# A two-block transformer kernel: the two norms around the first residual summed in four partition blocks, the first attention head's start reordered, and one buffer fill spread over two heads

## The reference, cut to what matters

```python
x = x + _rms_norm(mix, norm_post_mix[i])      # y = mix * rsqrt(mean(mix^2) + eps) * g
h = _rms_norm(x, norm_pre_ffn[i])
hid = h @ ffn_up                               # 1024 -> 2 * 2816
```

```python
q = (rms_norm(q_lat, g_qa) @ w_qb)             # per head 64 plain + 32 rotary columns
kv = (rms_norm(kv_lat, g_kva) @ w_kvb)         # per head 64 key + 64 value columns
q = concat([q_nope, rope(q_pe)]); k = concat([k_nope, broadcast(rope(k_pe))])
p = softmax(q @ k^T * scale); o = p @ v
```

## Time and profile before

| | us |
|---|---|
| median of 3 runs | 1794.77 |
| lowest and highest | 1790.65 to 1795.23 |
| the profiled execution | 1791.69 |
| its span, first to last instruction | 1789.8 |
| PE busy | 1745.0 (97%) |
| POOL, DVE, ACT busy | 954.3, 1026.1, 763.2 |
| mean granted clock of TensorE | 0.993 of full speed |

### The profile page before, as it was taken

How to read it: one execution, slowest core, us unless ns; L and a number is a source line. 1 busy time by engine, 2 the same in 40 slices (tenths; PEclk the granted TensorE clock), 3 DMA queues, 4 the chain that set the end, 5 groups by cost and what they waited for, 6 DMA issues and landing times.

```text
span 1789.8 us, 24548 instructions
## 1 busy us (share of the span) xinstructions
PE 1745.0 (97%) x9450; PEld 1401.5 (78%) x9450; DVE 1026.1 (57%) x1312; ACT 763.2 (43%) x1261; POOL 954.3 (53%) x758
## 2 busy tenths in 40 slices
PE   8999999999899999999998999999999999999997
PEld 7677999877488888887787777776867888888776
DVE  4697544576755555201455666667485666666575
ACT  4553766423333333101433565567124444444562
POOL 3443777757088999999356022224544444444062
PEclk9999999999999999999999999999999999999998
DMA  5121000224112222424111000001231111111221
GB/s 190 71 94 48 2 1 2 96 104 170 56 70 97 101 105 95 165 105 166 48 48 71 24 24 1 24 0 60 106 153 48 42 48 47 49 47 48 77 71 47
DMA packets 18861, 126.24 MB, mean 71 GB/s; under 512 B 2096, under 2 KB 2352, under 8 KB 4304
## 3 DMA queue, kind: packets, MB, share of 16 engines
q1 hardware_dynamic: 18624, 124.41, 18.8%
q10 hardware_dynamic: 144, 0.52, 0.1%
HBM read 122.83 MB, written 2.10 MB: 70 GB/s over the span
## 4 chain that ended last, share of the span: by engine, by line
PE 64%; issue 15%; POOL 11%; DVE 7%; ACT 2%; DMA 0%; POOLq 0%; ACTq 0%; SPq 0%; DVEq 0%
POOL w_hi L648 8%; PE banks L903 6%; PE banks L1231 5%; PE banks L1210 4%; PE banks L1382 4%; PE banks L1385 4%; PE banks L1383 4%; POOL w_lo L639 3%; PE banks L769 3%; PE banks L1093 3%; PE banks L1098 3%; PE banks L1094 3%; PE banks L1437 2%; PE banks L751 2%; PE banks L752 2%
## 5 line engine op out<-in xcount | busy, mean ns | idle before, releaser
L648 POOL TENSOR_TENSOR w_hi<-raw,der 128x512 fp32r<-128x512 f32 x296 | 342.6, 1168 | 462.1 <-PE banks L1385 187.3
L639 POOL TENSOR_TENSOR w_lo<-raw,w_hi 128x512 fp32r<-128x512 f32 x336 | 467.0, 1402 | 67.2 <-ACT w_hi L1528 67.2
L751 PE MATMUL banks<-h_hi,w_hi 128*128 128x512 f32 x496 | 197.5, 398 | 2.4 <-DVE h_lo L2363 2.2
L752 PE MATMUL banks<-h_lo,w_hi 128*128 128x512 f32 x496 | 193.2, 389 | 0.0
L753 PE MATMUL banks<-h_hi,w_lo 128*128 128x512 f32 x496 | 193.1, 389 | 0.0
L1382 PE MATMUL banks<-h_hi,w_hi 128*128 128x512 f32 (+1 forms) x384 | 145.5, 379 | 0.0
L1383 PE MATMUL banks<-h_lo,w_hi 128*128 128x512 f32 (+1 forms) x384 | 130.6, 355 | 0.0
L2011 ACT ACTIVATE dP<-banks,der 128x768 f32<-128x768 f32 x64 | 57.7, 902 | 160.8 <-DVE der L2767 160.8
L751 PEld LDWEIGHTS banks<-h_hi,w_hi 128*128 128x128 f32 x496 | 93.1, 188 | 31.9 <-issue 8.8
L1385 PE MATMUL banks<-h_hi,w_lo 128*128 128x512 f32 (+1 forms) x384 | 116.0, 356 | 0.0
L698 POOL TENSOR_TENSOR Of<-Of,Ls 128x768 f32<-128x768 f32 x8 | 14.6, 1831 | 186.9 <-DVE Ls L2569 186.9
(11 more groups left out here) (491 smaller groups left out, 4229.3 us busy)
## 6 DMA issues: line engine op xcount, KB each, us to landing
raw<-in_stream SPq DMA_DIRECT2D x84, 1024.0 KB, 4.8
ada_raw<-in_ada_w SPq DMA_DIRECT2D x18, 1024.0 KB, 6.9
raw<-in_ada_w SPq DMA_DIRECT2D x4, 1024.0 KB, 4.8
xT<-in_x_t SPq DMA_DIRECT2D x2, 1024.0 KB, 6.5
xT<-in_x_t SPq DMA_DIRECT2D x1, 2048.0 KB, 7.6
ada_end<-in_ada_w SPq DMA_DIRECT2D x2, 1024.0 KB, 5.8
out_t<-z SPq DMA_DIRECT2D x8, 256.0 KB, 2.1
ctxT<-in_ctx_t SPq DMA_DIRECT2D x1, 1024.0 KB, 7.1
```

What stands on the lines that cost most here:

```text
L639: return pool.tensor_tensor(lo[:, h, part(i), :], raw_tiles(half)[:, part(i), :], hi[:, h, part(i), :], ALU.subtract)
L648: pool.tensor_tensor(hi[:, h, part(i), :], raw_tiles(half)[:, part(i), :], one, ALU.mult).then_inc(hi_done, 1)
L751: pe.matmul(banks[b][:, :], hi, tile(rhs_hi, k), start=(at_k == 0), stop=False)
L752: pe.matmul(banks[b][:, :], hi, tile(rhs_lo, k), start=False, stop=False)
```

## The change

Norms: the squares of 7 tiles are added in `nacc`; the sum over partitions is made in four blocks of 128 tokens, each on 32 partitions (`block_sums`: four matmuls with 32 columns of ones), first of `nacc`, then of the eighth square directly from `nt`, whose tile ACT now squares before it copies it. Root and reciprocal are then taken of 128x128 numbers (`brs`), and `spread_blocks` brings them back to 512 columns in bank 5 with four matmuls, from where DVE reads them. The second norm is made likewise. Ada blocks 6 and 7 follow the first spread, block 8 stands between the fourth and the fifth square, and block 9 is cut in two halves around the second spread. The first block of the feed-forward projection is written out ahead of the loop: for each k the three matmuls of tile 0 and of tile 1. The four mask columns that the spread uses get columns of their own (`MASK`).

Attention: `tops(0, t)` stand behind k = 0 to 4 of `mla_in(11)` and `row(0)` behind k = 6. ACT's `row_copy(0)` comes before the last gate and `query_hi(1)`; its two `KHI[1]` copies move behind `weigh_keys(0, 2)`, and the two `KLO[1]` copies, formerly on DVE, behind `weigh_keys(0, 3)`. DVE takes all five reductions of head 0 before `rope_query(1)`; the fill of the second pair is cut into `fill_zeros` and `fill_ones`, for buffer 0 in head 0 and buffer 1 in head 1, and `query_lo(1)` moves behind `top(1, 0)`. PE's `query(2, 0)` moves ahead of `tops(1, 0)`.

```diff
@@ ada_blocks, PE
-        def ada_blocks(blocks):
+        def ada_blocks(blocks, parts=range(KT)):
...
-                for k in range(KT):
+                for k in parts:
...
@@ PE, the norms and the first feed-forward block
-        pe.wait_ge(out_summed, KT)
-        pe.matmul(banks[4][:, :], ones, nacc[:, :], start=True, stop=True).then_inc(post_sum, 1)
+        def block_sums(at, squares, first, last):
+            for j in range(4):
+                mm = pe.matmul(banks[4][32 * j:32 * j + 32, at:at + P], ones[:, 0:32], squares[:, P * j:P * j + P], start=first, stop=last)
+            return mm
+        def spread_blocks(root):
+            for j in range(4):
+                mm = pe.matmul(banks[5][:, P * j:P * j + P], der[:, MASK + j:MASK + j + 1].broadcast_to([P, P]), root, start=True, stop=True)
+            return mm
+        pe.wait_ge(out_summed, KT - 1)
+        block_sums(0, nacc, True, False)
+        pe.wait_ge(out_sq, KT)
+        block_sums(0, nt[:, 1, :], False, True).then_inc(post_sum, 1)
+        pe.wait_ge(post_root, 2)
+        spread_blocks(brs[:, 0, :]).then_inc(post_sum, 1)
         ada_blocks((6, 7))
         for k in range(KT):
+            if k == CT:
+                ada_blocks([8])
             pe.wait_ge(pre_sq, k + 1)
-            pe.matmul(banks[5][:, :], ones, nt[:, k % 2, :], start=(k == 0), stop=(k == KT - 1)).then_inc(pre_sq_read, 1)
-        ada_blocks((8, 9))
+            block_sums(P, nt[:, k % 2, :], k == 0, k == KT - 1).then_inc(pre_sq_read, 1)
+        ada_blocks([9], range(CT))
+        pe.wait_ge(pre_root, 2)
+        spread_blocks(brs[:, 1, :]).then_inc(pre_sq_read, 1)
+        ada_blocks([9], range(CT, KT))
+        n = STREAM["up"]
+        s = half_of(n)
+        pe.wait_ge(split_full, n + 1)
...
+        for k in range(KT):
+            pe.wait_ge(nh_ready, k + 1)
+            for j in range(2):
...
+                pe.matmul(b[:, :], hi, h1_hi[:, k, :], start=(k == 0), stop=False)
+                pe.matmul(b[:, :], hi, h1_lo[:, k, :], start=False, stop=False)
+                mm = pe.matmul(b[:, :], lo, h1_hi[:, k, :], start=False, stop=(k == KT - 1))
...
@@ PE, attention
-            if k in (0, 2, 3, 5, 6):
-                tops(0, (0, 2, 3, 5, 6).index(k))
-        row(0)
+            if k < 5:
+                tops(0, k)
+            if k == 6:
+                row(0)
...
+                if h == 0 and j == 0:
+                    query(after, 0)
@@ ACT, norms
-            if m < 2 * KT - 1:
+            if m % KT < KT - 1:
                 act.activation(out, banks[bank][:, :], ACT.Copy).then_inc(out_copied, 1)
...
-        act.activation(nr[:, :], banks[4][:, :], ACT.Sqrt, scale=1.0 / D, bias=der[:, 127:128]).then_inc(post_root, 1)
+        act.activation(brs[:, 0, :], banks[4][:, 0:P], ACT.Sqrt, scale=1.0 / D, bias=der[:, 127:128]).then_inc(post_root, 1)
...
@@ DVE, norms
-            chain.link(dve.reciprocal(nr[:, :], nr[:, :]))
+            dve.reciprocal(brs[:, 0, :], brs[:, 0, :]).then_inc(post_root, 1)
+            dve.wait_ge(post_sum, 2)
...
@@ DVE, attention
         for h in range(A_HEADS):
             nxt, after = h + 1, h + 2
             if nxt < A_HEADS:
                 top(nxt, 0)
+            if h == 0:
+                query_lo(1)
...
             if nxt < A_HEADS:
                 top(nxt, 1)
+            if h < 2:
+                fill_zeros(1, h)
...
             if nxt < A_HEADS:
                 top(nxt, 3)
+            if h < 2:
+                fill_ones(1, h)
```

More of the change, by code:

```diff
@@ L1044, in _ @@
+        n = STREAM["up"] + 1
+        project([2 * half_of(n), 2 * half_of(n) + 1], half_of(n), n, n // 2 + 1, h1_hi, h1_lo)
+        with pe.Fori(0, N_UP // 2 - 1) as i:
             for u in range(2):
                 s = half_of(STREAM["up"] + u)
-                n = 2 * i + (STREAM["up"] + u)
-                project([2 * s, 2 * s + 1], s, n, i + (STREAM["up"] + u) // 2 + 1, h1_hi, h1_lo, ready=None if u else nh_ready)
+                n = 2 * i + (STREAM["up"] + 2 + u)
+                project([2 * s, 2 * s + 1], s, n, i + (STREAM["up"] + 2 + u) // 2 + 1, h1_hi, h1_lo)
@@ L1275, in _ @@
                 if after < A_HEADS:
-                    if j in (0, 2):
+                    if j in (0, 2) and h + j:
                         query(after, j // 2)
@@ L1726, in _ @@
         act.wait_ge(pre_sq_read, KT)
-        act.activation(nr[:, :], banks[5][:, :], ACT.Sqrt, scale=1.0 / D, bias=der[:, 127:128]).then_inc(pre_root, 1)
+        act.activation(brs[:, 1, :], banks[4][:, P:2 * P], ACT.Sqrt, scale=1.0 / D, bias=der[:, 127:128]).then_inc(pre_root, 1)
         for k in range(KT):
@@ L1892, in _ @@
         query_copy(1)
+        row_copy(0)
         mla_gate(11)
         query_hi(1)
-        for e in range(2):
-            ins = act.activation(KHI[1][e][rope_rows(e), :], KHI[0][e][rope_rows(e), :], ACT.Copy)
-        ins.then_inc(kpe_high.sem, 1)
-        row_copy(0)
         weigh_keys(0, 0)
@@ L1910, in _ @@
             weigh_keys(h, 2)
+            if h == 0:
+                for e in range(2):
+                    ins = act.activation(KHI[1][e][rope_rows(e), :], KHI[0][e][rope_rows(e), :], ACT.Copy)
+                ins.then_inc(kpe_high.sem, 1)
             if h == A_HEADS - 1:
@@ L1913, in _ @@
             weigh_keys(h, 3)
+            if h == 0:
+                act.wait_ge(*kpe_low.at(1))
+                for e in range(2):
+                    ins = act.activation(KLO[1][e][rope_rows(e), :], KLO[0][e][rope_rows(e), :], ACT.Copy)
+                ins.then_inc(kpe_low.sem, 1)
             if h == A_HEADS - 1:
@@ L2418, in _ @@
         dve.wait_ge(pre_root, 1)
-        chain.link(dve.reciprocal(nr[:, :], nr[:, :]))
+        dve.reciprocal(brs[:, 1, :], brs[:, 1, :]).then_inc(pre_root, 1)
+        dve.wait_ge(pre_sq_read, KT + 1)
         for k in range(KT):
@@ L2504, in _, with fill_zeros, fill_ones @@
                                  op0=ALU.mult, op1=ALU.mult).then_inc(lat_normed, 1)
-        def fill(i):
-            for e in range(2):
-                c = slice(96, 128) if e == 0 else slice(0, 32)
-                dve.memset(KHI[i][e][c, :].bitcast(F32), 0.0)
-                dve.memset(KLO[i][e][c, :].bitcast(F32), 0.0)
-                ins = dve.memset(VV[i][e][:, :, 64 - 64 * e:128 - 64 * e], 1.0)
-            chain.link(ins)
-            for e in range(2):
-                ins = dve.memset(KHI[i][e][top_at(e):top_at(e) + 1, :].bitcast(F32), 1.0)
-            ins.then_inc(mla_filled.sem, 1)
+        def fill_zeros(i, e):
+            c = slice(96, 128) if e == 0 else slice(0, 32)
+            dve.memset(KHI[i][e][c, :].bitcast(F32), 0.0)
+            dve.memset(KLO[i][e][c, :].bitcast(F32), 0.0)
+            chain.mark(dve.memset(VV[i][e][:, :, 64 - 64 * e:128 - 64 * e], 1.0))
+        def fill_ones(i, e):
+            chain.wait()
+            dve.memset(KHI[i][e][top_at(e):top_at(e) + 1, :].bitcast(F32), 1.0).then_inc(mla_filled.sem, 1)
         dve.wait_ge(*kpe_high.at(1))
@@ L2528, in _ @@
             dve.memset(qf[e][swap_rows(e), :], 0.0)
-        fill(0)
+        fill_zeros(0, 0)
+        fill_zeros(0, 1)
+        fill_ones(0, 0)
+        fill_ones(0, 1)
         def rope_query(h):
@@ L2574, in _ @@
         query_lo(0)
+        for t in range(5):
+            top(0, t)
         rope_query(1)
         rope_query_sum(1)
-        for t in range(5):
-            top(0, t)
         dve.wait_ge(block_done, BLK_LAST + 1)
-        fill(1)
-        query_lo(1)
-        for e in range(2):
-            r = rope_rows(e)
-            ins = dve.tensor_copy(KLO[1][e][r, :], KLO[0][e][r, :])
-        ins.then_inc(kpe_low.sem, 1)
         for h in range(A_HEADS):
```

51 lines of the change are left out of this document (29 added, 22 removed).

## The result

The changed kernel takes 1781.70 us in the median of five runs (1781.49 to 1783.92), the kernel before 1794.77 (1790.63 to 1795.23) beside it. The ratio is 0.9937, with a 95% interval from 0.9924 to 0.9950: faster by 0.6%, and inside the range, 0.7 us above its lower end. A later repeat gave 1783.6 (ratio 0.9942, 0.9927 to 0.9957). The profiled execution took 1783.92 us, its span 1781.8 against 1789.8.

The account below looks back on a forecast made before the run. PE's queue was taken to bound the kernel; norms 5.1 us (6.8 less 1.7 for the clock) plus attention 3.9 (5.6 less 1.7) gave 9.0, 1782.7 us, plus 3.1 for the median: 1785.8, range 1781 to 1790.5.

Parts of the forecast that it names:

- What bounds the kernel: Whole kernel: PE, busy 97% of the span, sets the end, so gains on its queue at either place reach the end.
- Short form of the norms: Norms to first feed-forward block: DVE's products start 3.3 us earlier, `nh` 2.2, block ends 487.4 not 494.2; 6.8 us gained.
- The clock at the first norm: First norm, ada blocks 6 and 7: one fall to half speed for 3.4 us costs 1.7, leaving the norms 5.1 us.
- rival 1: First norm: the clock does not fall, so the gain is 10.7 us, 1784.1; chance 0.25.
- Head 0: Start of attention's heads: scores start 3.6 us earlier, full clock kept, `tops(1, 1)` at 982.5 instead of 988.05; 5.6 us gained.
- What is given back: Heads 0 and 1: DVE's memsets and rotary steps delay reductions by 0.8 us a head, 1.7 with row-copy delay; attention 3.9.
- Rival 3: Heads 0 and 1: DVE's fills cost 2.3 us per head, not 0.8; attention 0.9, together 6.0, 1788.8; chance 0.10.
- The sum: Whole kernel: norms 5.1 plus attention 3.9 gives 9.0 us; 1782.7 from the profiled execution, 1785.8 as median; chance 0.42.
- Rival 4: Norms: head start lost on PE's queue, `nh` at 475.0, block ends no earlier than 490.5; 5.0 us in all, 1789.8; chance 0.10.
- rival 5: First norm: the clock falls and ada products don't restore it; `nh` near 488.7, 5.1 us slower or up to 1800.5; chance 0.05.

Follow-up runs that it names:

- gap_filled: Changed kernel with the first four of ada block 8's eight matmuls moved ahead of PE's wait for the first spread; median 1783.3 us, ratio 0.9941.
- longer_idle: Changed kernel with a second 128x128 reciprocal on DVE ahead of the first norm's own, lengthening PE's gap; median 1784.65 us, ratio 0.9948.
- not_interleaved: Changed kernel with the first feed-forward block back in the loop, all of tile 0 before tile 1; median 1787.2 us, ratio 0.9966.
- row_copy_late: Changed kernel with ACT's row_copy(0) again behind the last gate and query_hi(1), key copies left as changed; median 1788.2 us, ratio 0.9966.
- fills_on_gpsimd: Changed kernel with the second pair's fills taken from DVE and put on POOL behind its split; median 1779.6 us, ratio 0.9922.
- before_again: The kernel before, unedited, run once more for a second trace; norms' interval 42.47 us instead of 41.54, heads' interval 52.28.
- again: The changed kernel, unedited, run once more as the reference; 1783.6 us, ratio 0.9942.

## Why the prediction was right, step by step

**What bounds the kernel.** Right. PE's queue is the late one at the norms: a gap filled in it came out whole in the interval (`gap_filled`), a gap widened in it as well (`longer_idle`). That the gains reach the end is borne out by the corrected spans, to some 1 us.

**Short form of the norms.** Right to 0.3 us at these steps, when the trace's start is shifted by the 0.9 us by which tile 7 was early: spread expected at 455.4 less 0.9, came at 454.54; `nh` 473.3, came at 472.98; split 486.5, came at 486.70. Reading the scale from a bank cost nothing: 748 ns an operation beside 752 in the earlier trace rows.

**The clock at the first norm.** This is the step that failed. The forecast took one fall for 1.7 us; in the traces of the changed kernel there was none, so rival 1 held (10.7 us). The size was right, 1.7 both in `not_interleaved` and in `longer_idle`, and so was the remark that a gap of this size has both outcomes. Wrong was to let the longer light stretch decide for a fall: of the eight traces with the short norms and their gap unfilled it fell in two, one of them with the lengthened gap; of the four with the long norms, in one. The Trainium skill, "TensorE: Matmul & The Clock Gate", section "Part 1: The HAM clock gate", says the windows run free of the kernel; 1.62 us with and without a fall, and 1.90 us likewise, agree with it. So the honest forecast was the kernel's time without falls plus a part of 1.7 us, and no choice of one outcome.

**Head 0.** Right in mechanism and in size: `tops(1, 1)` came 5.8 us sooner behind `tops(0, 0)` where 5.6 were predicted, no gap before the scores, 0.67 us before the values (0.9 predicted), full clock throughout. `row_copy_late` shows that the row copy's place carries it.

**What is given back.** 1.1 us, not 1.7. The term was mis-sized and not misnamed: `fills_on_gpsimd` got 1.17 back by taking exactly these memsets from DVE. Rival 3 (4.6 us over both heads) falls with it. Attention is 4.7 us instead of 3.9. Counted from `tops(1, 1)`, the changed kernel reaches `tops(1, 3)` when `fills_on_gpsimd` does (4.84 us), `tops(1, 4)` 0.3 us later than it, `row(1)` 0.9, `tops(2, 0)` 0.8 and `tops(3, 0)` 1.2 later. So the waits stand where the prediction had them and head 0 has its size, 0.8; head 1 gave back 0.4 more instead of another 0.8.

**The sum.** 6.7 + 4.7 = 11.4 us against 9.0: 1.7 of the difference is the clock, 0.8 the heads, less 0.1 in the norms. Against the median of before that is 1783.4; the measured 1781.7 lies 1.7 us lower, and no run says why. The forecast of 1785.8 was 4.1 us too high, and that the result still lay inside the range, by 0.7 us, is in part luck. The forecast also added 3.1 us because the trace of before lay that far under its median. That distance doesn't carry over: the median of before (1794.8) lay in the upper of its two groups and the trace near the lower, and the trace of the changed kernel lies 2.2 us above its own median. Rival 4 fell with `nh` at 473.0, and rival 5 with the windows of 456 to 459: the ada products brought the clock back where it fell (1.00 again at 459 to 461 in `not_interleaved`).

## What to carry to other kernels

Measure a place by an interval between two events on the busiest engine that enclose it; here it repeated to 0.1 us wherever the clock stayed up, while the whole time of one kernel moved by 4 to 6. Where a consumer at full rate waits for a producer at half rate, give it the second tile's work at each step rather than after the last; here that was the larger part of the norms' gain. And when a wait disappears, look at what DVE or ACT did under its cover: the memsets of the second pair cost nothing before, 2.1 us in their old place with the wait gone, 1.1 spread over two heads, and nothing on POOL, which was idle.

## What the runs showed of the hardware

The clock does not follow the length of the idle time before it. It was 0.50 behind 1.62 us (`not_interleaved`), 1.90 (`before_again`), 2.44, 2.61 and 2.69, and stayed 1.00 behind 1.62, 1.90, 2.69, 2.70 and even 3.03 us. It also fell with hardly any idle time or none: at 838.3 in the kernel after, behind 0.57 us, and at 1310.2 in `again`, where PE had been busy throughout, mostly with products of a single column. PE's timelines of the kernel after and of `again`, and a window of `again`:

```profile
837.02 1.16 PE L1033 MATMUL banks<-sq_c,der 128*128 128x128 f32 x8 [0.57 <-DVE der L2507]
```

```profile
1306.96 1.40 PE L1027 MATMUL banks<-sq_c,zacc 128*128 128x1 f32 x12
1308.21 1.48 PE L1027 MATMUL banks<-sq_c,zqacc 128*128 128x1 f32 x12
```

```profile
1310.00:1312.00 2.00, 2.00 (x7) 0.82 (x5) 2.00 (x4) 0.26 (x1) 2.00 (x3) 0.54 1.03 432
```

Outside the two intervals and the end of the run the falls stand at five places only: near 177 (in 5 of the 14 traces), 838 (3), 1310 (4), 1364 and 1682 (7 each). The last two fell in the same seven traces and in neither place in the other seven, although the idle time before them, some 2.7 and 1.7 us, was the same in all; so the outcome is not drawn anew at each place. Each fall lasted 3.4 us, or twice that behind the 3.97 us of head 0 in the kernels with the old start.

A stretch at 1.2 GHz costs what its place makes of it: 1.7 us in the norms of the changed kernel, where PE is late, 0.9 in those of the kernel before (`before_again`), where DVE's chain is, and some 1.5 elsewhere by the table above.

A memset of 32x768 took 0.73 us on POOL and 0.70 on DVE, and the one of 128x384 took 0.42 and 0.38, so POOL's pace in the split (1.04 us for 512 columns) doesn't hold for a memset: from 979.08 four took 2.8 us where the expectation had 5.4.

The load of ACT's table took 1.28 us at 972.69 in the kernel after and the exponential began at 973.98: nothing stood between them.
